# One five-slot ring for the split weights of a diffusion block, with the feed-forwards written out

## The reference, cut to what matters

```python
def ffn_sublayer(s, m, g_norm, w_in, w_out):      # w_in 1024 x 5632, w_out 2816 x 1024
    h = rmsnorm(s, g_norm) * (1.0 + m[1]) + m[0]
    g, u = jnp.split(h @ w_in, 2, axis=-1)
    return s + 0.5 * m[2] * ((silu(g) * u) @ w_out)

mod   = silu(c)     @ w_ada[l] + b_ada[l]         # 9 x 1024 values for the latent tokens
mod_c = silu(c_ctx) @ w_ada[l] + b_ada[l]         # and as many for the context tokens
```

## Time and profile before

| | |
|---|---|
| median of three runs | 2789.78 us |
| profiled execution, span from first to last instruction | 2794.2 us |
| TensorE busy in the span | 2513.9 us (90%) |
| VectorE busy | 1407.5 us (50%) |
| ScalarE busy | 865.7 us (31%) |
| GpSimd busy | 381.9 us (14%) |
| mean granted clock of TensorE | 0.942 |
| HBM read | 290.81 MB, 108 GB/s over the span |

### The profile page before, as it was taken

How to read it: one execution, slowest core, us unless ns; L and a number is a source line. 1 busy time by engine, 2 the same in 40 slices (tenths; PEclk the granted TensorE clock), 3 DMA queues, 4 the chain that set the end, 5 groups by cost and what they waited for, 6 DMA issues and landing times.

```text
span 2794.2 us, 37154 instructions
## 1 busy us (share of the span) xinstructions
PE 2513.9 (90%) x13996; PEld 2114.7 (76%) x13996; DVE 1407.5 (50%) x2290; ACT 865.7 (31%) x1303; POOL 381.9 (14%) x372
## 2 busy tenths in 40 slices
PE   5999898989989898989989889999998878888898
PEld 5777676886669686767767678878797677878888
DVE  4777766513342434567776743332343444345444
ACT  1433212333431213242221143322424421135543
POOL 2000003001130411200000300001001233121001
PEclk9999998889989999989999989999998988999999
DMA  5455444111110104245545422223321201034444
GB/s 230 147 181 183 147 154 151 53 61 35 57 57 1 57 23 152 97 150 181 180 159 188 156 76 98 93 79 97 113 76 60 65 29 40 10 113 145 154 147 137
DMA packets 96458, 302.82 MB, mean 108 GB/s; under 512 B 10592, under 2 KB 17504, under 8 KB 95584
## 3 DMA queue, kind: packets, MB, share of 16 engines
q1 hardware_dynamic: 76912, 229.69, 24.7%
q0 software_dynamic: 18720, 69.21, 7.6%
q10 hardware_dynamic: 720, 2.44, 0.2%
HBM read 290.81 MB, written 10.49 MB: 108 GB/s over the span
## 4 chain that ended last, share of the span: by engine, by line
PE 70%; DVE 11%; issue 9%; ACT 5%; POOL 3%; DMA 1%; DVEq 0%; ACTq 0%; POOLq 0%
PE ps L1404 17%; PE ps L1406 15%; PE ps L1405 15%; PE ps L1681 3%; PE ps L1672 3%; DVE w_lo L979 3%; DVE ps L1013 3%; ACT w_hi L620 3%; PE ps L1688 2%; PE ps L1579 2%; PE ps L1600 1%; PE ps L1511 1%; PE ps L1370 1%; PE ps L1726 1%; PE ps L1522 1%
## 5 line engine op out<-in xcount | busy, mean ns | idle before, releaser
L1404 PE MATMUL ps<-h_hi,w_hi 128*128 128x512 f32 (+1 forms) x2000 | 753.5, 377 | 82.0 <-DVE w_lo L979 41.7
L1405 PE MATMUL ps<-h_lo,w_hi 128*128 128x512 f32 (+1 forms) x2000 | 730.9, 365 | 0.0
L1406 PE MATMUL ps<-h_hi,w_lo 128*128 128x512 f32 (+1 forms) x2000 | 729.7, 365 | 0.0
L979 DVE TENSOR_TENSOR w_lo<-raw,w_hi 128x1024 fp32r<-128x1024 f32 (+2 forms) x368 | 417.5, 1141 | 561.2 <-ACT w_hi L620 545.2
L620 ACT ACTIVATE w_hi<-raw 128x1024 fp32r<-128x1024 f32 (+2 forms) x416 | 404.2, 974 | 738.3 <-PE ps L1406 735.6
L1404 PEld LDWEIGHTS ps<-h_hi,w_hi 128*128 128x128 f32 x2000 | 388.9, 194 | 169.0 <-DVE w_lo L979 53.4
L1406 PEld LDWEIGHTS ps<-h_hi,w_lo 128*128 128x128 f32 x2000 | 388.0, 194 | 58.8
L1405 PEld LDWEIGHTS ps<-h_lo,w_hi 128*128 128x128 f32 x2000 | 389.4, 195 | 54.0
L1404 PE MATMUL ps<-a_hi,w_hi 128*128 128x512 f32 (+1 forms) x960 | 357.7, 373 | 75.5 <-DVE w_lo L979 50.3
L1406 PE MATMUL ps<-a_hi,w_lo 128*128 128x512 f32 (+1 forms) x960 | 353.5, 368 | 0.0
L1405 PE MATMUL ps<-a_lo,w_hi 128*128 128x512 f32 (+1 forms) x960 | 351.7, 366 | 0.0
(11 more groups left out here) (200 smaller groups left out, 2597.2 us busy)
## 6 DMA issues: line engine op xcount, KB each, us to landing
raw<-in_w_up SPq DMA_DIRECT2D x176, 512.0 KB, 3.8
ada<-in_w_ada_t POOLq DMA_DIRECT2D x128, 512.0 KB, 3.7
raw<-in_w_down SPq DMA_DIRECT2D x64, 384.0 KB, 3.2
raw<-in_w_gate SPq DMA_DIRECT2D x48, 512.0 KB, 3.7
raw<-in_w_down SPq DMA_DIRECT2D x64, 320.0 KB, 2.9
raw<-in_w_proj SPq DMA_DIRECT2D x32, 512.0 KB, 3.5
raw<-in_w_merge SPq DMA_DIRECT2D x16, 512.0 KB, 3.8
raw<-in_w_out SPq DMA_DIRECT2D x16, 512.0 KB, 3.5
```

Of the source, the lines that this page charges most:

```text
L979: vec.tensor_tensor(w_lo[:, j % SPLIT, 0:cols], raw[:, j, 0:cols], w_hi[:, j % SPLIT, 0:cols].bitcast(F32), ALU.subtract).then_inc(s_lo, 1)
L1404: pe.matmul(out, wh, rows_hi[:, i, 0:n], start=first, stop=False)
L1405: pe.matmul(out, wh, rows_lo[:, i, 0:n], start=False, stop=False)
L1406: return pe.matmul(out, wl, rows_hi[:, i, 0:n], start=False, stop=last)
```

## The change

The two-slot `w_hi`, the two-slot `w_lo` and the four-slot `raw` become one ring of five slots, in which `w_lo` lies over `raw`: the subtraction writes over the loaded words. Block b always uses slot b modulo 5. A load waits until TensorE is done with block b-5, and a cast waits for nothing but the landing. Casts and lower parts are issued in block order, up to four blocks ahead of the block that is multiplied in a feed-forward, three ahead in a norm (four in the first) and one or two in a mixer. The feed-forwards are written out without loops on all engines. The down phase starts when the first 6 pieces of `a_lo` are there, and its later chunks wait for 12, 17 and 22. The modulation tiles are spread 48, 48 and 32 over feed-forwards 0, 1 and 2. Single sums stand between the other instructions of VectorE, write straight to where they are kept, and end in the down phase's first two tiles; the values are made from them after its third tile. One of the two `ada` slots moves behind `a_lo`. In the mixers `rms` is replaced by other scratch space and the numbering of blocks follows the ring; the order of instructions stays. Of the diff, cut:

```diff
-RAW, SPLIT = 4, 2
+RING = 5
+AHEAD = RING - 1
...
 ADA_REST = DEPTH * ADA - ADA_FIRST
-ADA_PART = tuple(2 * KF + KD * z for z in ADA_DOWN)
-assert sum(ADA_PART) == ADA_REST and ADA_PART[0] % 2 == 0
+ADA_PART = (48, 48, 32)
+assert sum(ADA_PART) == ADA_REST
...
+FFN_COLS = [KD * P] * (2 * KF) + [(k1 - k0) * P for _ in range(KD) for k0, k1 in CHUNKS]
+COLS = FFN_COLS + [KD * P] * N_MIX + FFN_COLS + FFN_COLS + [KD * P] * N_MIX + FFN_COLS
...
-        raw = sb("raw", [P, RAW, KD * P])
-        w_hi = sb("w_hi", [P, SPLIT, KD * P], F32R)
-        w_lo = sb("w_lo", [P, SPLIT, KD * P], F32R)
-        ada = sb("ada", [P, 2, KD * P])
+        with ExitStack() as s:
+            raw = sb("raw", [P, RING, KD * P], at=s)
+        w_lo = sb("w_lo", [P, RING, KD * P], F32R)
+        w_hi = sb("w_hi", [P, RING, KD * P], F32R)
+        ada_a = sb("ada_a", [P, KD * P])
...
-        rms = sb("rms", [P, TOK])
-        inv = sb("inv", [P, TOK])
+        rms = sb("rms", [P, 80])
+        inv = sb("inv", [P, 80])
...
+            ada_b = sb("ada_b", [P, KD * P], at=s)
...
         def mods_at(l, which):
 
-            return ((1, 3, 3), (4, 4, 4))[l][which]
+            return ((1, 3, 3), (5, 5, 6))[l][which]
...
-            def load(j, b, src, cols=KD * P, wait=True):
-
-                if wait:
-                    sp.wait_ge(s_lo, b - RAW + 1)
-                sp.dma_start(raw[:, j, 0:cols], src).then_inc(s_raw[j], 16)
+            def load(b, src):
+
+                if b >= RING:
+                    sp.wait_ge(s_pe, b - RING + 1)
+                sp.dma_start(raw[:, b % RING, 0:COLS[b]], src).then_inc(s_raw[b % RING], 16)
...
-                with sp.Fori(1 if f == 0 else 0, KF // 2) as it:
-                    up(it)
-                with sp.Fori(0, KD) as i:
-                    for j, (k0, k1) in enumerate(CHUNKS):
-                        load(j, b0 + 2 * KF + 4 * i + j, a["w_down"][f, i, :, k0 * P:k1 * P], (k1 - k0) * P)
+                for n in range(2 * KF):
+                    load(b0 + n, a["w_up"][f, n])
+                for i in range(KD):
+                    for m, (k0, k1) in enumerate(CHUNKS):
+                        load(b0 + 2 * KF + 4 * i + m, a["w_down"][f, i, :, k0 * P:k1 * P])
...
             def load_ada(f):
 
...
-                    load(it)
+                for t in range(sum(ADA_PART[:f]), sum(ADA_PART[:f + 1])):
+                    if t >= 2:
+                        pool.wait_ge(s_adu, 2 * t - 2)
+                    pool.dma_start(ada[t % 2][:, :], a["w_ada_t"][ADA_FIRST - KD + t]).then_inc(s_ada[t % 2], 16)
...
             load_ada(1)
             squares(3, TOK)
+            load_ada(2)
             squares(4, TOK)
...
-            def cast(j, b, cols=KD * P, free=True):
-
-                if free:
-                    act.wait_ge(s_pe, b - SPLIT + 1)
-                return act.activation(w_hi[:, j % SPLIT, 0:cols], raw[:, j, 0:cols], ACT.Copy)
...
+            cast_next = [0]
+
+            def casts(end):
+
+                for b in range(cast_next[0], end):
+                    j, n = b % RING, COLS[b]
+                    act.wait_ge(s_raw[j], 16 * (b // RING + 1))
+                    act.activation(w_hi[:, j, 0:n], raw[:, j, 0:n], ACT.Copy).then_inc(s_hi, 1)
+                cast_next[0] = max(cast_next[0], end)
...
                 if 0 < s < 6:
-                    casts()
+                    casts(STAGE_BASE[s] + AHEAD - 1)
                 act.wait_ge(*tile_ready(s, KD - 1))
...
                 if s == 0:
-                    casts()
+                    casts(AHEAD)
...
-                with act.Fori(0, KF // 2 - 1) as it:
-                    pair(2 * it + 1, 1, it)
-                    pair(2 * it + 2, 0, it + 1)
-                pair(KF - 1, 1, KF // 2 - 1)
-                silu, upper = finish(KF - 1, 1)
-                silu()
-                upper()
-                with act.Fori(0, KD) as i:
-                    for j, (k0, k1) in enumerate(CHUNKS):
-                        landed(j, b0 + 2 * KF, i)
-                        cast(j, b0 + 2 * KF + 4 * i + j, (k1 - k0) * P).then_inc(s_hi, 1)
+                for q in range(KF):
+                    casts(b0 + 2 * q + AHEAD)
+                    silu(q)
+                    casts(b0 + 2 * q + AHEAD + 1)
+                    upper(q)
+                for i in range(KD):
+                    for m in range(4):
+                        casts(min(b0 + 2 * KF + 4 * i + m + AHEAD, len(COLS)))
...
-                def lowers():
-                    for j in range(2):
-                        lower(j, STAGE_BASE[s] + j)
                 if 0 < s < 6:
-                    lowers()
+                    lowers(STAGE_BASE[s] + AHEAD - 1)
                 vec.wait_ge(s_rt, s + 1)
                 vec.reciprocal(inv[:, 0:n // P], rms[:, 0:n // P]).then_inc(s_inv, 1)
                 if s == 0:
                     modulations(0, 0, 2)
-                    lowers()
+                    lowers(AHEAD)
                 vec.wait_ge(s_bc, s + 1)
...
-            def lower(j, b, cols=KD * P):
-
-                vec.wait_ge(s_hi, b + 1)
-                vec.tensor_tensor(w_lo[:, j % SPLIT, 0:cols], raw[:, j, 0:cols],
-                                  w_hi[:, j % SPLIT, 0:cols].bitcast(F32), ALU.subtract).then_inc(s_lo, 1)
+            lower_next = [0]
+
+            def lowers(end):
+
+                for b in range(lower_next[0], end):
+                    j, n = b % RING, COLS[b]
+                    vec.wait_ge(s_hi, b + 1)
+                    vec.tensor_tensor(w_lo[:, j, 0:n], raw[:, j, 0:n], w_hi[:, j, 0:n].bitcast(F32),
+                                      ALU.subtract).then_inc(s_lo, 1)
+                lower_next[0] = max(lower_next[0], end)
...
+                def hidden(q):
                     vec.wait_ge(s_pe, b0 + 2 * q + 2)
                     vec.wait_ge(s_silu, p0 + q + 1)
-                    vec.tensor_tensor(buf_b[:, j, 0:n], buf_a[:, j, 0:n], ps[:, 2 * j + 1, 0:n],
+                    vec.tensor_tensor(buf_b[:, q % 2, 0:n], buf_a[:, q % 2, 0:n], ps[:, 2 * (q % 2) + 1, 0:n],
                                       ALU.mult).then_inc(s_mul, 1)
+
+                def hidden_low(q):
                     vec.wait_ge(s_ahi, p0 + q + 1)
-                    vec.tensor_tensor(a_lo[:, q, 0:n], buf_b[:, j, 0:n], a_hi[:, q, 0:n].bitcast(F32),
+                    vec.tensor_tensor(a_lo[:, q, 0:n], buf_b[:, q % 2, 0:n], a_hi[:, q, 0:n].bitcast(F32),
                                       ALU.subtract).then_inc(s_alo, 1)
...
-                                                           ada_sum[:, 2 * j + i:2 * j + i + 1]).then_inc(s_adu, 1)
-                    vec.wait_ge(s_adu, 4 * r + 4)
-                    vec.tensor_copy(mod_rest[:, r, :], ada_sum[:, :]).then_inc(s_adc, 1)
-                    vec.wait_ge(s_adc, r + 1)
...
+                part = 0 if f == 3 else ADA_PART[f]
+                ada0 = sum(ADA_PART[:f])
+
+                def modulate(u):
+
+                    if u >= 2 * part:
+                        return
+                    t, i = ada0 + u // 2, u % 2
+                    vec.wait_ge(s_ada[t % 2], 16 * (t // 2 + 1))
+                    if t or i:
+                        vec.wait_ge(s_adu, 2 * t + i)
+                    vec.tensor_tensor_reduce(ps[:, 6:8, :].rearrange("p b n -> p (b n)"), ada[t % 2][:, :],
+                                             c_wide[:, i, :], 1.0, 0.0, ALU.mult, ALU.add,
+                                             mod_rest[:, t // 2, 2 * (t % 2) + i:2 * (t % 2) + i + 1]).then_inc(s_adu, 1)
+
+                def sums_kept(t):
+
+                    vec.wait_ge(s_adu, 2 * t)
 
                 if f < 2:
                     vec.wait_ge(s_wact, f + 1)
-                with vec.Fori(0, KF // 2 - 1) as it:
-                    pair(2 * it + 1, 1)
-                    pair(2 * it + 2, 0)
-                pair(KF - 1, 1)
-                finish(KF - 1, 1)
-                if f < 2:
-                    modulate(ada0 // 2 + KF - 1)
+                for q in range(KF):
+                    lowers(b0 + 2 * q + AHEAD)
+                    modulate(4 * q)
+                    if q:
+                        hidden_low(q - 1)
+                    modulate(4 * q + 1)
+                    lowers(b0 + 2 * q + AHEAD + 1)
+                    modulate(4 * q + 2)
+                    hidden(q)
+                    modulate(4 * q + 3)
+                hidden_low(KF - 1)
                 bd = b0 + 2 * KF
-
-                def turn(it, j, first=False):
-
-                    i = 2 * it + j
...
+                if f == 0:
+                    sums_kept(KD)
+                    modulations(0, 2, 3)
+                if f == 1:
+                    sums_kept(ADA_PART[0] + KD)
+                    modulations(0, 8, 9)
+                if f == 2:
+                    sums_kept(ADA_REST)
+                    modulations(1, 5, 9)
+                for i in range(KD):
+                    for m in range(4):
```

(46 more changed lines are left out.)

147 lines of the change are left out of this document (42 added, 105 removed).

## The result

The changed kernel takes 2659.96 us, the median of four runs from 2655.67 to 2671.62, against 2790.17 for the kernel before beside it (2789.26 to 2791.2). The ratio is 0.954, with a 95% interval from 0.9519 to 0.9561: 130.2 us less. Two executions of all, one of 9474.77 us of the kernel shifted by 32 bytes in experiment 7 and one of 3248.45 us of the kernel before, fell in a slow state and are left out.

What follows compares the result with a forecast made beforehand. It took TensorE, busy 2513.9 of 2794.2 us, and its waits, the largest for VectorE's lower weight parts, as the bound. 129.4 - 2.45 + 2.8 = 129.7 us off gave 2664.5, less 4.4 gave 2660 us; range 2640 to 2698.

Steps and rivals of the forecast that it cites:

- What removes the waits: In the feed-forwards, five slots let casts run up to four blocks ahead, so TensorE's waits go: 129.4 us over eight phases.
- Feed-forward 3: Last feed-forward, on 256 tokens: at TensorE's own pace its up phase saves 18.4 us and its down phase 7.0.
- The lead is kept: In up phases with sums, VectorE needs 9.3 us a pair against TensorE's 10.9, leaving 1.5 us for hand-offs.
- The start: First norm: four lower parts instead of two before the scaling of x, with TensorE idle behind them, cost 2.45 us.
- The clock behind removed waits: Norms behind feed-forwards 0 and 1: without a long wait just before, 1.4 us less each, 2.8 us more saved.
- Mixers at nothing: In the mixers, the order of instructions is kept, so no gain or cost was counted.
- The last step: Whole kernel: the median of the runs stands 4.4 us below the profiled span, taken off 2664.5 to give 2660 us.
- VectorE did not become the bound: Rival, up phases with sums: hand-offs of 2 us make each pair 0.5 us late, 30 us in all: 2690; chance 0.10.
- The short ring: Rival, feed-forward 3: ring too short for short blocks, so 13 + 7 us stay: 2680; chance 0.08.
- The clock: Rival, start of stages: 3.4 us of matmul time comes back in each of four or five: 2645; chance 0.08.
- The up-to-down waits: Rival, between up and down phases: the 9.22 us wait and its like stay in three or four places: 2692; chance 0.04.
- The instruction stream: Rival, written-out feed-forwards: 62 more instruction packets, TensorE stalling 3.4 us for each, 211 us: 2871, slower; chance 0.04.

Runs made afterwards that it cites:

- experiment 7: Changed kernel with a_hi, a_lo and all behind rms moved: by 32 bytes ratio 0.9581, by 64 2650.59 us, by 96 2658.79; only a_hi moved 2662.05, only a_lo 2653.84.
- Experiment 2: The changed kernel with a lead of two blocks instead of four, casts again waiting for TensorE to finish the block two before: 2686.32 us, ratio 0.9627.
- experiment 3: The changed kernel with the four sums of a pair in a row behind a_lo, as before the change: 2659.26 us, ratio 0.9542.
- experiment 6: The changed kernel with the modulation sums over feed-forwards 0 and 1 only (60 and 68 tiles), instead of 48, 48 and 32 over three: 2671.33 us, ratio 0.9588.
- experiment 1: The kernel before with every hardware loop of its feed-forwards written out and nothing else changed: 2752.02 us, ratio 0.9867.
- experiment 8: The changed kernel with arrays moved by 64 bytes, feed-forward 3's four operands 64 bytes further on, and two lower parts in the first norm: 2655.94 us, ratio 0.9511.

## Why the prediction was right, and where it was not

**The whole.** 2660 us was predicted, 2659.96 measured, and the closeness is luck. The span was predicted at 2664.5 us and came at 2669.8, 5.3 us too low. The median was to lie 4.4 us below the span and lay 9.8 below, 5.4 us more. The two errors cancel. What was right is the mechanism and its main term: the eight phases give 132.7 us, predicted 129.4.

**The phases on 512 tokens** are right to within 1 us each: 43.4, 50.7 and 7.6 us against 44.2, 51.4 and 8.4. Taking TensorE's pace from stretches without a wait and multiplying it by the count of matmuls is what made this hold, where the waits alone, 92 us, would have fallen short by nearly a third: the phases gave 132.7.

**What removes the waits.** The prediction gave the lead of five slots as what takes them away, and read the 9.22 us between up and down as also the fault of two slots. Experiment 2 keeps a lead of two blocks and has at most 0.7 us in that place, so the order of the work does more than the slots: 66.2 of the 132.7 us against 35.9, with 30.6 for the loops. With the lead there, single sums are worth nothing (experiment 3), so lead and order can in part stand in for each other. What writing the loops out is worth comes for the most part (25.5 us) from shorter waits for VectorE, a part of the sum that the prediction did not set apart.

**Feed-forward 3 was mis-sized:** predicted 18.4 + 7.0 = 25.4, measured 19.4 + 11.6 = 31.0. The steps were "1008 x 0.121" and "528 x 0.122". The pace is 120.0 ns in both phases of the kernel before (for the down phase see the two lines in experiment 7), so about 1 us in each phase is a pace taken too slow. The other 3.6 us come because the down phase after runs at 113.3 ns: `a_hi` and `a_lo` begin elsewhere in the changed kernel, which is the layout's doing and not the ring's, and which the prediction did not have.

**The lead is kept.** VectorE fits its work into 10.9 us a pair with no wait of TensorE. It is busy for 180.2 of 228.5 us, 8.6 a pair: the 9.3 add durations that partly overlap, and the third up phase shows 67% where up to about 85% was forecast. The reason given, sums between the steps, was not needed (experiment 3). The distribution over three feed-forwards is worth 17 us in the norms (experiment 6), which the prediction did not name: it had only noted that the sums' end no longer falls into the last chunks; it did not follow GpSimd's queue to the squares.

**The start** costs 1.8 us of the predicted 2.45. TensorE's wait for the first `h_lo` grew from 4.36 to 6.63, and the wait of 2.20 for `w_lo` behind the first two blocks went, which counts in the up phase; with two lower parts the first is 4.36 again. This wait of the kernel after:

```profile
68.33 0.77 PE L1376 MATMUL ps<-h_hi,w_hi 128*128 128x512 f32 x1 [6.63 <-DVE h_lo L941]
```

**The clock behind removed waits** was predicted at 2 x 1.4 us and came at 1.4 + 0 (the norm behind feed-forward 1 takes 24.4 us in both). Here the reason fell, not just the size: experiment 1 keeps a long wait ahead of the window and takes 23.2 us, and the kernel moved by 64 bytes has none and takes 24.4:

```profile
430.20:454.60 24.40, 18.67 (x75) 15.85 (x75) 11.69 (x22) 16.01 (x29) 0.00 (x0) 0.72 0.32 109
```

The window takes 21.9 to 24.5 us in kernels with the same work in it, as the mean granted clock goes from about 0.85 to 0.72.

**Mixers at nothing** was wrong for this profile by 9.0 us in mixer 1. In all profiles together mixer 0 takes either 674 to 681 or 688 to 690 us, and mixer 1 either 533 to 537 or 542 to 545, with no change in its work except for the place of `a_hi` (2 or 3 us). The long forms have a lower mean clock. The long form of mixer 0 is in the kernel before too: its 689.4 us. Its waits there are no longer than those of the short form; from 311 to 351 us of the mixer the clock is 0.64 in the kernel before and 0.85 in that of experiment 1, and why is open.

The long form of mixer 1 begins with a wait. VectorE makes two pieces of `vnew` just as GpSimd starts on the lower part of a weight block. In the kernel after, and then in that of experiment 6:

```profile
2376.26 2.65 DVE L1246 TENSOR_TENSOR vnew<-em,vtmp 128x128 f32<-128x128 f32 x2
2376.41 2.35 POOL L512 TENSOR_TENSOR w_lo<-raw,w_hi 128x1024 fp32r<-128x1024 f32 x1 [7.11 <-ACT w_hi L617]
2379.06 0.65 PE L1687 MATMUL ps<-q_dec,state 64*64 64x128 f32 x2 [2.10 <-DVE vnew L1246]
```

```profile
2377.46 0.49 DVE L1249 TENSOR_TENSOR vnew<-em,vtmp 128x128 f32<-128x128 f32 x2
2377.66 2.50 POOL L512 TENSOR_TENSOR w_lo<-raw,w_hi 128x1024 fp32r<-128x1024 f32 x1 [7.16 <-ACT w_hi L617]
```

In the first GpSimd starts 0.15 us behind VectorE and in the second 0.20. In the first the second piece of `vnew` ends only after GpSimd does, and TensorE waits 2.10 us. In the 14 profiles this wait and the long form of mixer 1 go together: six have both, eight neither; GpSimd starts 0.12 to 0.19 us behind in the six and 0.19 to 0.21 in the eight. The kernel moved by 64 bytes and the last version of experiment 8 reach this place equally late, within 0.1 us; the first has the wait and takes 542.8 us for the mixer, the second has not and takes 536.3. The mixer up to there and from there on, in the kernel after and in the kernel before:

```profile
1918.90:2376.20 457.30, 404.52 (x2985) 357.27 (x2986) 192.93 (x386) 123.19 (x232) 88.95 (x66) 0.90 0.16 48
2376.20:2462.40 86.20, 70.02 (x502) 65.12 (x500) 47.33 (x76) 36.16 (x53) 24.71 (x19) 0.84 0.50 159
```

```profile
2020.90:2474.50 453.60, 400.60 (x2987) 353.54 (x2986) 194.21 (x387) 123.95 (x233) 89.01 (x66) 0.91 0.15 47
2474.50:2555.40 80.90, 67.27 (x502) 63.33 (x500) 44.59 (x74) 35.31 (x51) 23.57 (x19) 0.92 0.52 169
```

So 5.3 of the 9.0 us come from there on, the wait and a clock of 0.84 instead of 0.92 behind it, and 3.7 before it. That the wait pulls the clock down is argued from this order; no run was made to remove it.

**The last step, 4.4 us from the profile to the median,** was taken as fixed and is not. A run's time is its span and 1.8 us. By that the profiled execution of before was 5.8 us longer than the median of its runs (2788.4), and the one after, the longest of its four, 11.6 us longer than theirs (2658.2). So 124.4 us between the profiles and 130.2 between the medians are the same change. Of the 5.3 us by which the span was predicted too low, mixer 1 is 9.0 and the first windows 1.4, against 3.3 from the phases (5.6 too little predicted in the last feed-forward, 2.3 too much in the others) and under 2 from the start and the rest.

**The rivals.** VectorE did not become the bound. The short ring had no wait; with four slots waits begin. The clock gave 1.4 us and not more than the 2.8 of the forecast. The up-to-down waits are gone; with the old `a_lo` wait 2.6 us come back, not 9.22. The instruction stream took 36 packets more, not 62, and in no phase is TensorE idle. The rule weighed in the prediction (the Trainium skill, Runtime: NRT & Kernel Launch, Instruction fetch mechanics) says that the fetch of straight code is mostly hidden; the trace agrees, with TensorE busy for all of 228.5 us in an up phase. A stall at a taken branch, which it also names, no run shows: what writing the loops out gave in experiment 1 lies for the most part in shorter waits for VectorE (25.5 us) and in mixer 0's form (12.5). For experiment 6 the Trainium skill (GPSIMD Engine Reference, Specifications) says that GpSimd's way to SBUF is shared with VectorE and contended by VectorE instructions with two SBUF inputs; 1288 ns going to 1849 beside the sums agrees.

**Open:** what decides in an execution which form mixer 0 takes, and what shifts GpSimd against VectorE by the few hundredths of a microsecond that decide for mixer 1; why the pace hangs on the begin of both arrays; whether 64 bytes behind a multiple of 256 would give 113 ns in the up phase too, which was not tried.

## What to carry to other kernels

Read an engine's own pace from stretches without waits, times its count of instructions, and compare phase by phase; waits alone understate what goes with them. Give the buffers of a hand-off chain a few blocks of lead before polishing the order inside a pair, and look at what else stands in the queue of an engine that issues loads. Before a gain under 0.5% is believed or denied, compare the windows of stages that were not changed: here mixers with the same work move by 9 to 14 us.

## What the runs showed of the hardware that was not expected

- The begin of the moving operands changes a matmul's pace with no wait recorded: 226.5 to 234.5 ns on 512 tokens, 113.3 to 120.0 on 256 (experiment 7), some 10 us of this kernel for three phases when both begin at a multiple of 128.
- Stages with the same instructions take one of two durations some 10 us apart (mixer 0: 676.9 at a clock of 0.94, 689.4 at 0.92), and kernels of one computation differ in spread: 2 us in the four runs of the kernel before beside the changed one (10 over 26 executions), 16 in the changed one, 21 in the last version.
- Two short VectorE instructions take 2.65 us instead of 0.49 when a 2.35 us instruction of GpSimd starts 0.15 us behind the first of them, and not when it starts 0.20 us behind; mixer 1 takes 542.8 us with such a wait and 536.3 without, in two kernels that reach the place equally late.
- A table load that stands once in a loop's turn is executed in every turn, 1.28 us each; written out, the count of table loads falls from 55 to 28.
